# Expert coefficients: every second group of four tokens gets bare one-hots from VectorE in one compare, its gates from GpSimd

## The reference, cut to what matters

```
q = (h @ w_query).reshape(B, S, 8, 2, 128)
s1, s2 = scores of the two halves against 128 sub-keys each
v1, i1 = top_k(s1, 16);  v2, i2 = top_k(s2, 16)
cand = v1[..., :, None] + v2[..., None, :]            # 256 sums per head
top_v, pos = top_k(cand, 16)
expert_idx = i1 * 128 + i2 at pos                     # 16 of 16384 experts per head
gates = softmax(top_v)
act = gelu(h . expert_down[expert_idx])
out = sum over heads and picks of gates * act * expert_up[expert_idx]
```

## Time and profile before

| | |
|---|---|
| three runs | 1890.52, 1895.82, 1896.05 us (median 1895.82) |
| the profiled execution | 1896.35 us, of which the span of the trace 1895.0 us |
| TensorE busy | 1728.0 us (91%) |
| VectorE busy | 1121.1 us (59%) |
| ScalarE busy | 461.1 us (24%) |
| GpSimd busy | 384.9 us (20%) |
| mean granted TensorE clock | 0.956 of full speed |

### The profile page before, as it was taken

How to read it: one execution, slowest core, us unless ns; L and a number is a source line. 1 busy time by engine, 2 the same in 40 slices (tenths; PEclk the granted TensorE clock), 3 DMA queues, 4 the chain that set the end, 5 groups by cost and what they waited for, 6 DMA issues and landing times.

```text
span 1895.0 us, 25552 instructions
## 1 busy us (share of the span) xinstructions
PE 1728.0 (91%) x10111; PEld 1289.2 (68%) x10111; DVE 1121.1 (59%) x2297; ACT 461.1 (24%) x825; POOL 384.9 (20%) x241
## 2 busy tenths in 40 slices
PE   6998998998899957869988888899999999999998
PEld 2333554543455447537888888788888888888887
DVE  4774223331243263425992399967778777777776
ACT  1003232121122221111355555511111111111111
POOL 0000000000000110000276422233333333333332
PEclk9999999999899779889999899999999999999999
DMA  9974333333733100142233321245544555454453
GB/s 342 334 269 164 121 120 115 108 134 119 239 111 133 45 1 3 57 148 89 94 111 121 100 72 68 80 170 179 183 165 156 186 171 183 170 173 169 164 173 112
DMA packets 120523, 267.75 MB, mean 141 GB/s; under 512 B 10210, under 2 KB 43346, under 8 KB 120276
## 3 DMA queue, kind: packets, MB, share of 16 engines
q1 hardware_dynamic: 86352, 228.82, 35.0%
q10 hardware_dynamic: 34052, 37.29, 5.8%
HBM read 261.86 MB, written 4.22 MB: 140 GB/s over the span
## 4 chain that ended last, share of the span: by engine, by line
PE 78%; DVE 13%; issue 2%; ACT 2%; DMA 2%; POOL 1%; ACTq 0%; SPq 0%; DVEq 0%; POOLq 0%
PE bank L466 24%; PE bank L869 12%; PE bank L871 12%; PE bank L873 12%; PE bank L881 5%; DVE hot L1515 3%; PE bank L853 3%; DVE ada_acc L990 3%; DVE hot L1513 2%; POOL dT_low L1977 1%; PE bank L911 1%; PE bank L731 1%; PE bank L449 1%; DMA ada_b<-in_b_ada_dram 1%; PE bank L740 1%
## 5 line engine op out<-in xcount | busy, mean ns | idle before, releaser
L466 PE MATMUL bank<-slot,hT 128*128 128x512 f32 (+2 forms) x1088 | 477.9, 595 | 6.2 <-DVE hT L977 2.0
L466 PEld LDWEIGHTS bank<-slot,hT 128*128 128x128 f32 x1088 | 206.9, 194 | 247.2 <-issue 242.2
L1981 POOL TENSOR_TENSOR up_low<-slot,up_high 128x512 fp32r<-128x512 f32 x128 | 229.6, 1794 | 428.9 <-DVE up_high L1430 428.9
L869 PE MATMUL bank<-hT_high,dT_high 128*128 128x256 f32 x1024 | 296.4, 289 | 13.0 <-POOL dT_low L1977 13.0
L871 PE MATMUL bank<-hT_low,dT_high 128*128 128x256 f32 x1024 | 290.8, 284 | 0.0
L873 PE MATMUL bank<-hT_high,dT_low 128*128 128x256 f32 x1024 | 289.3, 283 | 0.0
L869 PE MATMUL bank<-up_high,A_high 128*128 128x512 f32 x512 | 206.2, 403 | 3.4 <-DVE A_low L1433 3.4
L869 PEld LDWEIGHTS bank<-hT_high,dT_high 128*128 128x128 f32 x1024 | 195.8, 191 | 17.5 <-issue 14.6
L871 PE MATMUL bank<-up_low,A_high 128*128 128x512 f32 x512 | 202.3, 395 | 0.0
L873 PE MATMUL bank<-up_high,A_low 128*128 128x512 f32 x512 | 201.6, 394 | 0.0
L1892 ACT CAST dT_high<-bank 128x512 fp32r<-128x512 f32 x256 | 143.9, 595 | 230.4 <-PE bank L881 226.1
(11 more groups left out here) (407 smaller groups left out, 2199.7 us busy)
## 6 DMA issues: line engine op xcount, KB each, us to landing
slot<-in_expert_down_dram SPq DMA_DIRECT2D x128, 512.0 KB, 4.5
slot<-in_expert_up_dram SPq DMA_DIRECT2D x128, 512.0 KB, 3.8
slot<-in_w_in_dram SPq DMA_DIRECT2D x27, 2048.0 KB, 8.0
P<-in_w_ada_dram ACTq DMA_DIRECT2D x24, 1024.0 KB
slot<-in_w_out_dram SPq DMA_DIRECT2D x4, 2048.0 KB, 7.8
slot<-in_w_query_dram SPq DMA_DIRECT2D x4, 2048.0 KB, 7.9
slot<-in_w_branch_sb_dram SPq DMA_DIRECT2D x2, 2048.0 KB, 7.8
slot<-in_w_branch_ret_dram SPq DMA_DIRECT2D x2, 2048.0 KB, 8.5
```

Source lines behind the costliest of these rows:

```text
L466: m = pe.matmul(sums, lhsT=lhs[:, k, t * P:(t + 1) * P], rhs=w[:, k, :], start=(k == 0), stop=(k == w.shape[1] - 1))
L869: pe.matmul(o, lhsT=lhs_high.bitcast(F32R), rhs=rhs_high.bitcast(F32R), start=start, stop=False, skip_group_check=True)
L1981: g.tensor_tensor(up_low[p % 4][:, CW:].bitcast(F32R), up_tile[p % 4][:, CW:], up_hi[p % 2][:, CW:], ALU.subtract).then_inc(up_low_pool, 1)
```

## The change: the diff

In groups 1 and 3 of every turn VectorE now makes both halves of `hot[u]` in one compare of 4 x 128 x 2 = 1024 columns, without gates. GpSimd then multiplies the first key's half by the gate, in place, in one instruction of 512 columns whose second operand is one gate per 128 columns. TensorE waits for that product in groups 1 and 3. Groups 0 and 2 are made as before; `hot_made` now counts those alone. In GpSimd's stream the two gate instructions of a turn stand ahead of the two `dT_low` instructions of the tile that TensorE turns after that turn's four groups.

```
@@ v_coefficients
-                v.tensor_tensor(hot[u][:, 1], iota4, selT[:, 1, at:at + 4].unsqueeze(2).broadcast_to([P, 4, P]), ALU.is_equal)
-                for n in range(4):
-                    m = v.tensor_scalar(hot[u][:, 0, n, :], iota, selT[:, 0, at + n:at + n + 1],
-                                        selT[:, 2, at + n:at + n + 1], ALU.is_equal, ALU.mult)
-                m.then_inc(hot_made, 1)
+                if u % 2:
+                    v.tensor_tensor(hot[u], iota8, selT[:, 0:2, at:at + 4].unsqueeze(3).broadcast_to([P, 2, 4, P]),
+                                    ALU.is_equal).then_inc(hot_bare, 1)
+                else:
...
+                    m.then_inc(hot_made, 1)
                 if turn:
                     v_apply(turn - 1, u)
@@ pe_made
-        pe.wait_ge(hot_made, 4 * turn + u + 1)
+        if u % 2:
+            pe.wait_ge(hot_gated, 2 * turn + u // 2 + 1)
+        else:
+            pe.wait_ge(hot_made, 2 * turn + u // 2 + 1)
@@ GpSimd
+    def g_gates(turn):
+        for u in (1, 3):
+            toks = slice(turn * 16 + 4 * u, turn * 16 + 4 * u + 4)
+            g.wait_ge(hot_bare, 2 * turn + u // 2 + 1)
+            g.tensor_tensor(hot[u][:, 0], hot[u][:, 0], selT[:, 2, toks].unsqueeze(2).broadcast_to([P, 4, P]),
+                            ALU.mult).then_inc(hot_gated, 1)
+
     def g_experts():
         g.wait_ge(x_out, 16)
         for n in range(AHEAD):
+            if n > EARLY:
+                g_gates(n - EARLY - 1)
             for k4 in range(2):
...
+        g_gates(MIDDLE - 1)
```

More of the change, by code:

```diff
@@ L164, in program @@
     gate_shifted, gate_exp, picks_ready = sem("gate_shifted"), sem("gate_exp"), sem("picks_ready")
+    hot_bare, hot_gated = sem("hot_bare"), sem("hot_gated")
     hot_made, c_copied, middle_out, middle_in = sem("hot_made"), sem("c_copied"), [sem(f"middle{j}_out") for j in range(2)], [sem(f"middle{j}_in") for j in range(2)]
@@ L438, in program @@
     iota4 = iota.unsqueeze(1).broadcast_to([P, 4, P])
+    iota8 = iota.unsqueeze(1).unsqueeze(1).broadcast_to([P, 2, 4, P])
     picks = [x.rearrange("p (t h) k -> p t (h k)", t=TT) for x in (sel_key[:, 0], sel_key[:, 1], gates)]
@@ L1512, in v_coefficients @@
                     held(v, ("made", turn - 1, u))
-                v.tensor_tensor(hot[u][:, 1], iota4, selT[:, 1, at:at + 4].unsqueeze(2).broadcast_to([P, 4, P]), ALU.is_equal)
-                for n in range(4):
-                    m = v.tensor_scalar(hot[u][:, 0, n, :], iota, selT[:, 0, at + n:at + n + 1],
-                                        selT[:, 2, at + n:at + n + 1], ALU.is_equal, ALU.mult)
-                m.then_inc(hot_made, 1)
+                if u % 2:
+                    v.tensor_tensor(hot[u], iota8, selT[:, 0:2, at:at + 4].unsqueeze(3).broadcast_to([P, 2, 4, P]),
+                                    ALU.is_equal).then_inc(hot_bare, 1)
+                else:
+                    v.tensor_tensor(hot[u][:, 1], iota4, selT[:, 1, at:at + 4].unsqueeze(2).broadcast_to([P, 4, P]), ALU.is_equal)
+                    for n in range(4):
+                        m = v.tensor_scalar(hot[u][:, 0, n, :], iota, selT[:, 0, at + n:at + n + 1],
+                                            selT[:, 2, at + n:at + n + 1], ALU.is_equal, ALU.mult)
+                    m.then_inc(hot_made, 1)
                 if turn:
```

## The result

The changed kernel takes 1904.7 us (median of 6 runs, 1899.98 to 1906.56) against 1895.1 for the kernel before: a ratio of 1.0056, interval 1.0042 to 1.0070. A second comparison later gave 1.0070 (1.0056 to 1.0083). It is slower by 0.6%, some 10 us. 1906.2 us was predicted. The profiled execution has a span of 1903.2 us.

What follows compares the result with a forecast made beforehand. VectorE was taken to bound the coefficient stage: 6.78 + 1.84 + 0.77 + 0.85 = 10.24 us a turn against 9.60. 15 x 0.64 - 0.08 + 0.81 = +10.3 us gave 1906.2 us, range 1894 to 1917.

Steps and rivals of the forecast that it cites:

- The saving: VectorE in groups 1 and 3: compare plus four gated one-hots, 1.63 us, become one 1.14 us compare, saving 0.98 us a turn.
- The gate's length: Each new GpSimd multiply of 512 columns takes 1.04 us alone, bounds 1.04 and 1.27 us.
- Rival C: Much slower: each GpSimd gate takes 1.27 us and blocks VectorE in full, +21 us, 1917 us; chance 0.20.
- The 0.1 us from a bare compare to its gate: Estimated delay between the end of VectorE's ungated compare and the start of GpSimd's multiply, about 0.1 us.
- The gates' price to VectorE: VectorE stalls beside GpSimd's new multiplies: 0.77 us for group 3 and 0.85 us for group 1, each turn.
- VectorE stays the bound: In the coefficient stage, VectorE's 10.24 us turn exceeds TensorE's 7.9 us of work and the 8.65 us GpSimd loop.
- the loop through GpSimd: Per turn 3.08 us to the dT_low pair, 2.58 pair, 1.04 group 1 gate, 1.95 two products: 8.65 us.
- Rival D: TensorE's loop takes over, growing from 8.65 to over 10.24 us; halved clock adds 1 to 3 us; no separate chance.
- the others: Outcomes outside the main case and the three rivals that were given chances of their own; chance 0.02.
- Beginning and end: First turn 6.44 us against 6.52, -0.08; TensorE's last product after the last turn starts later, +0.81 us.
- A, the wash: Gates fall beside VectorE's applies and cost 0.5 us each, cancelling the gain: +1 us, 1897 us; chance 0.18.
- B, no contention for the gate's form: Broadcast gates leave VectorE alone, only the pair stalls it; GpSimd's loop 8.65 us a turn, -13.5, 1882 us; chance 0.08.

## Why the prediction was right, and where it was not

*The saving.* The bare compare takes 1.21 us alone (1.14 from start to start), and the kernel without gates has a turn of 8.67 us against the 8.62 of the prediction. Right.

*The gate's length.* 1.04 us, from the one row with a broadcast operand; 1040 ns is what gates take where VectorE leaves them alone. Right for the instruction alone. Rival C took 1.27, and 1261 ns is indeed the mean in the changed kernel, but as a stretched length: the first of two gates shows 1.46 us and the second about 1.0. C's 1917 us did not come. The 0.1 us from a bare compare to its gate, for which no row was named, is 0.08 in the run with the gate of group 1 ahead (1138.12 + 1.21 to 1139.41).

*The gates' price to VectorE.* 0.77 and 0.85 us were predicted; 0.74 and 0.72 are what the run with the gate of group 1 ahead shows. In a full-clock turn of the changed kernel the two gates together stretch four one-hots from 1.10 to 2.57 us (1.47), and the pair costs 0.89 (bare compare) + 0.70 (compare), 1.59 for the 1.84 taken. Right in kind, a little high. The places were not as predicted: the gate of group 3 does not follow its bare compare at once, under an apply, but stands behind the pair and the gate of group 1.

*"VectorE stays the bound."* This step failed. I put the loop through GpSimd at 8.65 us. It is 9.96 at full clock. I had the two engines exclude each other but charged every stall to VectorE, while GpSimd kept its lengths of the earlier trace rows. In the changed kernel the 1024-column compare gets in ahead of the second `dT_low` instruction (pair 3.51 us in place of 2.58), and a one-hot ahead of the gate (1.46 in place of 1.04). The wait from gate to product, 0.14 us, is a further term that the loop had left out. From the start of the third product to the pair's start it is 2.9 us, near the 3.08 I used: 3.5 + 1.46 + 0.14 + 1.95 + 2.9 = 9.95. The half-clock stretches then hit TensorE while it was in the loop, +1.47 us in one turn of three, of which a shorter pair gives half back in the next. In the full-clock turn VectorE is busy 9.95 of 9.95 us, so up to there it is as much a bound as the loop; the rest of the 10.25 comes while VectorE waits: the three turns by windows have a mean of 10.22 us, with 9.48 of it busy on VectorE. Rival D had both parts, the loop and the halved clock; I had priced it at 1 to 3 us on top, and of the chances it had at most the 0.02 of the others.

*Why the sum still came out.* With VectorE alone as the bound, a turn is 10.20 us in the order of the run with the gate of group 1 ahead, and the loop gives 10.25 in the order of the change. The nearness of these two is chance. The prediction's 10.24 was right for a mechanism that was just as slow as the one at work, and that is luck. It would not have told what to do next either: GpSimd's order by itself gave nothing (10.20 us), the compares' stalls by themselves 0.75 us (9.50), and both together 1.42 (8.83).

*Beginning and end.* The first turn took 6.26 us (1079.24 - 1072.98) against 6.44 predicted, and the first pair came 1.4 us later, which I had not priced. The end cost 0.9 us against 0.81.

*Rivals.* A, the wash: a gate costs 0.66 to 0.74 us, not 0.5. B, no contention for the gate's form: refuted by the stretched compares; its 8.65 us a turn was passed only with all iota in PSUM. The Trainium skill's rule that the two engines exclude each other for the whole of an instruction (SBUF — State Buffer, Who interferes with whom) had given 10.2 to 11.4 us a turn. Where VectorE is the bound, in the run with the gate of group 1 ahead, 10.20 us sits at its lower end.

## What to carry to other kernels

Before work goes from VectorE to GpSimd, look at both engines' means beside the same instruction alone (for the 512-column compare 804 against 675 ns here). Where they differ, expect the move to add stalls on both engines, as it did here, and either may be the next bound. Price the exclusion in both directions, and walk every loop with the stretched lengths. If one operand of the stalled instructions can live in PSUM, try that first, and for every kind of them: with the compares alone the change, in the better order, was worth nothing (8.83 against 8.82 us a turn); with the one-hots too it went from 0.5% slower to 1.3% faster, each against the kernel before with the iota in the same place.

## What the runs showed that I had not expected

Putting one of two kinds of stalled instruction out of the other engine's way moved the stall to the kind that was left (mean 509 to 656 ns) and kept the whole of the change's loss (0.68 us a turn against 0.62). A gated one-hot of 128 columns takes 0.32 us from start to start with its iota in PSUM and 0.26 with it in SBUF, and this slower form was the better one. In the order with the gate of group 1 ahead of the pair the granted clock was 1.00 in 1085 to 1215 us, against 0.94 in the changed kernel, with TensorE busy 99.42 against 100.80 us and no gain in time. What makes the clock fall in one turn of three of the changed kernel, no run was made to show.
